# The reciprocal square root of every RMSNorm on 128x5 numbers, spread over the partitions by TensorE

## The chip, the core and the metric

The kernel runs on one core of one Trainium2 chip. The metric is device time in microseconds (us) of one execution; lower is better. The kernel below was timed three times and profiled once more.

## The reference

A two-layer encoder works on 576 tokens at once: 512 of a new stream (`x_prompt`) and 64 of a running one (`x_sample`), each of width 1024. Layer 0 mixes tokens by retention, layer 1 by forgetting attention; both have a half SwiGLU block before and after the mixer. Every projection reads a normalised stream, and one normalisation closes the model:

```python
def rmsnorm(x, g):
    xf = x.astype(jnp.float32)
    y = xf * lax.rsqrt(jnp.mean(xf * xf, axis=-1, keepdims=True) + EPS) * g.astype(jnp.float32)
    return y.astype(x.dtype)

def swiglu_ffn(h, g, w_in, w_out):
    gate, up = jnp.split(rmsnorm(h, g) @ w_in, 2, axis=-1)
    return (jax.nn.silu(gate) * up) @ w_out

h = h + 0.5 * swiglu_ffn(h, ffn1_g, ffn1_w_in, ffn1_w_out)
h = h + mixer(rmsnorm(h, mix_g))            # retention, or forgetting attention
h = h + 0.5 * swiglu_ffn(h, ffn2_g, ffn2_w_in, ffn2_w_out)
# after layer 0 also: k, v, gates = split(rmsnorm(h, kv_g) @ w_kvf)
```

## The kernel before

**Layout.** Activations are kept transposed: `h` is [128 partitions, 8 blocks of the width, 576 tokens], so tokens run along the free dimension. Each projection is cut into units. A unit is 128 output features for all 576 tokens: for each of `kt` blocks of the contraction, TensorE (PE) does three products of split float32 operands (`wl`·`xh`, `wh`·`xl`, `wh`·`xh`), each in two halves of 288 tokens, into two PSUM banks. With 8 blocks that is 48 matmuls. The weights come from HBM into `raw` (SyncE issues the loads), ScalarE (ACT) makes the high part `wh`, VectorE (DVE) the low part `wl`; there are two buffers of `wh`/`wl`, so `wh` of unit u waits for the end of unit u-2.

**The rings.** In the sections named q, k, v and in the retention projections a unit writes one of two pairs of banks (ring of 2), and unit u waits until DVE has taken unit u-2 out of PSUM (semaphore `taken`). In the feed-forward sections the ring has four pairs (`DEEP`). Where a section needs a norm, the sums use banks 4 and 5, so its third unit first waits for a step of the norm (`newton`).

**The norm.** The gain is applied to `h` before the product (`xh`, `xl`), the factor 1/rms after it, when DVE takes a unit out of PSUM: `gate`, `rt`, `kvt`, `qT` are all `ps * rstd`. So `rstd` must stand in SBUF as [128, 576], the same row in every partition. It is made beside the first units of a section:
- GpSimd (POOL) squares and adds the 8 blocks of `h` into `ssq` [128, 576] (L1019, L1023).
- After the first unit PE multiplies `ssq` by a matrix of ones, which sums over the partitions and leaves the sum in every partition (`sum_partitions`, L1195).
- DVE, once it has made `wl` of the third unit, does `make_rstd`: mean plus epsilon out of PSUM (L665), a seed by integer arithmetic (L666), and three Newton steps of three instructions each (L669, L670, L671), all on [128, 576] and each waiting for the one before it. Only then does it take the first unit.

This happens seven times: at the start of ffn1 of layer 0, of the retention projections (the first head only), of ffn2 of layer 0, of k, of q, of ffn2 of layer 1, and for the final norm, behind which there are no more units. ffn1 of layer 1 uses the `rstd` of k again. Below, the norm of ffn1, ffn2 and ffn2 of layer 1 are called norms 0, 2 and 5; those of the retention, k and q norms 1, 3 and 4; the final one is norm 6. The order of instructions on each engine is the order in which the code is written; there is no scheduler. In `section`, DVE and ACT split the weights of unit s+2 ahead of taking unit s.

Of the kernel before, what the change touches and what calls it, by code (L numbers as in the profile page):

```python
# [24 lines left out]
I32 = mybir.dt.int32  # L25
ALU = mybir.AluOpType
# [8 lines left out]
HT = T // 2  # L35
# [12 lines left out]
NEWTON_STEPS = 10  # L48
# [52 lines left out]
def encoder(nc, A, O):  # L101
# [22 lines left out]
    with ExitStack() as ctx:  # L124
# [21 lines left out]
        newt = sb("fixed", "newt", [P, T])  # L146
# [83 lines left out]
        def unit_psum(s, ring=2):  # L230
            return ps[:, 2 * (s % ring):2 * (s % ring) + 2, 0:HT]

        def halves(ap):
            return ap.rearrange("p (a t) -> p a t", a=2)
# [22 lines left out]
        newton = sem("newton")  # L257
        rstd_ready = sem("rstd_ready")
# [387 lines left out]
        def _(dve):  # L646
# [9 lines left out]
            def make_rstd():  # L656

                n_norm[0] += 1
                dve.wait_ge(msum_ready, n_norm[0])

                def step(instruction):
                    n_newton[0] += 1
                    instruction.then_inc(newton, 1)
                    dve.wait_ge(newton, n_newton[0])
                step(nc.vector.tensor_scalar(halves(sq[:, :]), ps[:, 4:6, 0:HT], 1.0 / D, EPS, ALU.mult, ALU.add))  # L665
                step(nc.vector.tensor_scalar(rstd[:, :].bitcast(I32), sq[:, :].bitcast(I32), -0.5, RSQRT_SEED,  # L666
                                             ALU.mult, ALU.add))
                for n in range(3):
                    step(nc.vector.tensor_tensor(newt[:, :], rstd[:, :], rstd[:, :], ALU.mult))  # L669
                    step(nc.vector.scalar_tensor_tensor(newt[:, :], newt[:, :], -0.5, sq[:, :], ALU.mult, ALU.mult))  # L670
                    last = nc.vector.scalar_tensor_tensor(rstd[:, :], newt[:, :], 1.5, rstd[:, :], ALU.add, ALU.mult)  # L671
                    if n < 2:
                        step(last)
                last.then_inc(rstd_ready, 1)
                dve.wait_ge(rstd_ready, n_norm[0])

            def take_h(u, s, j, scale, gain, ring=2):

                dve.wait_ge(unit_done, u + 1)
                nc.vector.scalar_tensor_tensor(halves(h[:, j, :]), unit_psum(s, ring), scale, halves(h[:, j, :]),  # L680
                                               ALU.mult, ALU.add).then_inc(taken, 1)
                if gain is not None:
                    x_tile(j, gain)
# [3 lines left out]
            def ffn(name, gain, factor=None):  # L687
                for part, (j0, n) in enumerate(FF_PARTS):
                    u0, u1, p0 = first[f"{name}_in{part}"], first[f"{name}_out{part}"], pairs[0]

                    def take_in(i, s):
                        b, a = s // 2, p0 + 2 * i + s // 2
                        dve.wait_ge(unit_done, u0 + 4 * i + s + 1)
                        if s % 2 == 0:

                            nc.vector.tensor_tensor(halves(gate[:, b, :]), unit_psum(s, DEEP), halves(rstd[:, :]), ALU.mult) \  # L696
                                .then_inc(taken, 1)
                        else:
                            dve.wait_ge(rsilu_ready, a + 1)
                            nc.vector.tensor_tensor(halves(prod[:, b, :]), unit_psum(s, DEEP), halves(rsilu[:, b, :]), ALU.mult) \  # L700
# [12 lines left out]
            nc.vector.memset(ones[:, :], 1.0).then_inc(setup, 1)  # L713
            dve.wait_ge(const_in, 16 * 8)
# [13 lines left out]
            def head(hd, first_head=False, last_head=False):  # L728
                u0 = RET + 20 * hd

                def scaled(out, s, factor):
                    nc.vector.scalar_tensor_tensor(halves(out), unit_psum(s), factor, halves(rstd[:, :]),
                                                   ALU.mult, ALU.mult).then_inc(taken, 1)
# [110 lines left out]
            def log_gates():  # L844

                dve.wait_ge(f_done, 1)
                step(nc.vector.tensor_tensor(halves(lz[:, :]), ps[0:FOX_HEADS, 4:6, 0:HT], halves(rstd[0:FOX_HEADS, :]),
# [30 lines left out]
            def take_kv(u0, n0):  # L878
                def take(i, s):
# [16 lines left out]
                    nc.vector.tensor_tensor(halves(kvt[:, s % 2, :]), unit_psum(s), halves(rstd[:, :]), ALU.mult) \  # L896
# [16 lines left out]
            def take_q(i, s):  # L913
                dve.wait_ge(unit_done, first["q"] + 4 * i + s + 1)
                nc.vector.scalar_tensor_tensor(halves(qT[:, 4 * i + s, :]), unit_psum(s), (D // FOX_HEADS) ** -0.5,
                                               halves(rstd[:, :]), ALU.mult, ALU.mult).then_inc(taken, 1)
# [241 lines left out]
        def _(pe):  # L1158
            def product(out, terms, start, stop):

                for n, (w, x) in enumerate(terms):
                    for a in range(2):
                        mm = nc.tensor.matmul(out[:, a, :], w, x[:, a * HT:(a + 1) * HT],  # L1163
                                              start=start and n == 0, stop=stop and n == len(terms) - 1)
# [25 lines left out]
            def sum_partitions():  # L1190
# [3 lines left out]
                for a in range(2):  # L1194
                    mm = nc.tensor.matmul(ps[:, 4 + a, 0:HT], ones[:, :], ssq[:, a * HT:(a + 1) * HT], start=True, stop=True)  # L1195
                mm.then_inc(msum_ready, 1)

            def units(name, mh, ml, arrives=None, norm=False, ring=2, after_two=True):
# [37 lines left out]
            pe.wait_ge(setup, 4)  # L1236
            ffn("ffn1_0")

            def head(hd, first_head=False):
                u0 = RET + 20 * hd  # L1240
                for s in range(12):
                    unit(u0 + s, s, KD, xh, xl, x_arrives() if first_head and s == 0 else None)
# [93 lines left out]
            for s in range(4):  # L1336
                unit(u0 + s, s, KD, xh, xl, x_arrives() if s == 0 else None)
# [10 lines left out]
            for k in range(KD):  # L1348
                mm = product(ps[:, 4:6, 0:HT], ((fwl[:, k, :], xh[:, k, :]), (fwh[:, k, :], xl[:, k, :]),
# [121 lines left out]
            sum_partitions()  # L1471

# [37 lines left out]
```

## Time and profile before

| | |
|---|---|
| three runs, us | 2776.21, 2769.71, 2768.78 (median 2769.71) |
| the profiled execution, us | 2764.16 |
| its span, first to last instruction, us | 2762.6 |
| mean granted clock of TensorE | 0.985 of full |
| busy share: PE, DVE, ACT, POOL | 95%, 40%, 24%, 14% |

Between the span and the profiled execution's time lie 1.6 us. The granted clock is 1 where PE runs at full speed (2.4 GHz) and 0.5 at its lower level (1.2 GHz).

### The profile page before, as it was taken

How to read it: one execution, taken by the hardware profiler on the slowest of the kernel's cores; microseconds unless marked ns; L12 is line 12 of the kernel's file. 1: busy time of each engine (PE TensorE's matmuls, PEld its weight loads, DVE VectorE, ACT ScalarE, POOL GpSimd, SP SyncE). 2: the span in 40 equal slices, each digit the busy share in tenths (PEclk: the TensorE clock that was granted, in tenths of full speed). 3: DMA queues.
4: the chain of work that ended last, by engine and by line, in shares of the span. 5: the costliest groups of instructions: out<-in, count | busy, mean ns of one | idle time of the engine just before them, and what ended most of it. 6: DMA issues, size and time to landing. Idle time of an engine off the chain costs nothing.

```text
span 2762.6 us, 44345 instructions
## 1 busy us (share of the span) xinstructions
PE 2624.5 (95%) x18595; PEld 2491.9 (90%) x18595; DVE 1107.2 (40%) x1543; ACT 671.0 (24%) x918; POOL 383.2 (14%) x329
## 2 busy tenths in 40 slices
PE   6999999999899999999999999999998899999995
PEld 5999999969696968999999999999996578999995
DVE  5332335444444446332334433323344545332333
ACT  2221222121212122221222232212213422221220
POOL 3110113101010103100112111001130012100112
PEclk9999999999999999999999999999999999999998
DMA  4232232222221213232233332322331222232220
GB/s 117 84 99 67 79 97 75 61 81 66 72 74 60 83 39 92 84 106 62 84 91 94 113 92 84 96 65 84 92 101 50 78 68 75 82 100 62 84 84 35
DMA packets 392550, 221.74 MB, mean 80 GB/s; under 512 B 8016, under 2 KB 384432, under 8 KB 392416
## 3 DMA queue, kind: packets, MB, share of 16 engines
q1 hardware_dynamic: 387120, 202.82, 25.2%
q0 software_dynamic: 5296, 16.94, 1.9%
q8 instruction: 108, 1.77, 0.3%
q14 instruction: 26, 0.21, 0.0%
HBM read 206.01 MB, written 13.71 MB: 80 GB/s over the span
## 4 chain that ended last, share of the span: by engine, by line
PE 87%; DVE 7%; ACT 2%; issue 1%; DMA 1%; SPq 0%; POOL 0%; DVEq 0%; ACTq 0%; POOLq 0%
PE ps L1163 80%; PE ps L1283 1%; DVE wl L453 1%; PE ps L1296 1%; PE ps L1380 1%; DVE xl L653 1%; PE ps L1271 1%; ACT wh L448 1%; DVE newt L669 1%; DVE rstd L671 1%; DVE newt L670 1%; PE ps L1424 1%; ACT xh L484 1%; DVE sc L921 0%; DVE rt L814 0%
## 5 line engine op out<-in xcount | busy, mean ns | idle before, releaser
L453 DVE TENSOR_TENSOR wl<-raw,wh 128x1024 fp32r<-128x1024 f32 (+3 forms) x352 | 456.9, 1298 | 1347.8 <-ACT wh L448 1347.7
L1163 PE MATMUL ps<-xh,wl 128*128 128x288 f32 x4096 | 885.3, 298 | 23.7 <-DVE xl L653 8.6
L1163 PE MATMUL ps<-xl,wh 128*128 128x288 f32 x4096 | 880.3, 297 | 0.0
L1163 PE MATMUL ps<-xh,wh 128*128 128x288 f32 x4096 | 879.6, 297 | 0.0
L1163 PEld LDWEIGHTS ps<-xh,wl 128*128 128x128 f32 x4096 | 663.9, 190 | 27.7 <-issue 20.1
L448 ACT CAST wh<-raw 128x1024 fp32r<-128x1024 f32 (+3 forms) x352 | 375.7, 1067 | 1263.2 <-PE ps L1163 1262.0
L1163 PEld LDWEIGHTS ps<-xl,wh 128*128 128x128 f32 x4096 | 664.0, 190 | 0.0
L1163 PEld LDWEIGHTS ps<-xh,wh 128*128 128x128 f32 x4096 | 663.6, 190 | 0.0
L1042 POOL TENSOR_TENSOR rsilu<-silu,rstd 128x576 f32<-128x576 f32 x88 | 125.4, 1426 | 1296.4 <-ACT silu L495 1296.4
L1163 PE MATMUL ps<-actl,wh 128*128 128x288 f32 x1408 | 302.0, 295 | 0.0
L1163 PE MATMUL ps<-acth,wh 128*128 128x288 f32 x1408 | 302.0, 295 | 0.0
L1163 PE MATMUL ps<-acth,wl 128*128 128x288 f32 x1408 | 301.9, 295 | 0.0
L1163 PEld LDWEIGHTS ps<-acth,wh 128*128 128x128 f32 x1408 | 225.5, 188 | 0.0
L1163 PEld LDWEIGHTS ps<-actl,wh 128*128 128x128 f32 x1408 | 225.5, 188 | 0.0
L1163 PEld LDWEIGHTS ps<-acth,wl 128*128 128x128 f32 x1408 | 225.5, 188 | 0.0
L495 ACT ACTIVATE silu<-gate 128x576 f32<-128x576 f32 x88 | 60.4, 687 | 197.2 <-DVE gate L696 197.2
L497 ACT CAST acth<-prod 128x576 f32 (+1 forms) x88 | 59.4, 675 | 182.8 <-DVE prod L700 182.8
L703 DVE TENSOR_TENSOR actl<-prod,acth 128x576 f32 (+1 forms) x88 | 66.7, 758 | 78.3 <-ACT acth L497 78.3
L1023 POOL TENSOR_TENSOR ssq<-ssq,sq 128x576 f32<-128x576 f32 x49 | 84.0, 1714 | 3.8
L680 DVE SCALAR_TENSOR_TENSOR h<-ps,h 128x576 f32<-128x576 f32 x104 | 78.0, 750 | 11.7 <-PE ps L1163 11.7
L1019 POOL TENSOR_TENSOR sq<-h 128x576 f32<-128x576 f32 x49 | 56.2, 1147 | 185.4 <-DVE h L680 183.4
L653 DVE SCALAR_TENSOR_TENSOR xl<-h,gains,xh 128x576 fp32r<-128x576 f32 x56 | 58.7, 1068 | 37.1 <-ACT xh L484 37.1
(202 smaller groups left out, 1628.3 us busy)
## 6 DMA issues: line engine op xcount, KB each, us to landing
raw<-in_ffn_w_in SPq DMA_DIRECT2D x176, 512.0 KB, 3.7
raw<-in_ffn_w_out SPq DMA_DIRECT2D x32, 768.0 KB, 4.8
raw<-in_ret_w_in SPq DMA_DIRECT2D x48, 512.0 KB, 3.8
raw<-in_ffn_w_out SPq DMA_DIRECT2D x32, 640.0 KB, 4.4
raw<-in_ret_w_out SPq DMA_DIRECT2D x32, 256.0 KB, 2.7
raw<-in_fox_w_kvf SPq DMA_DIRECT2D x16, 512.0 KB, 4.0
raw<-in_fox_w_q SPq DMA_DIRECT2D x8, 512.0 KB, 4.1
bias<-cum_scratch SPq DMA_DIRECT2D x16, 256.0 KB, 3.2
```

Source lines behind the costliest of these rows:

```text
L448: nc.scalar.copy(wh[:, s % SPLIT, 0:kt, :], raw[:, s, 0:kt, :]).then_inc(hi_ready, 1)
L453: nc.vector.tensor_tensor(wl[:, s % SPLIT, 0:kt, :], raw[:, s, 0:kt, :], wh[:, s % SPLIT, 0:kt, :].bitcast(F32), ALU.subtract).then_inc(lo ...
L484: nc.scalar.activation(xh[:, j, :], h[:, j, :], ACT.Copy, scale=gains[:, gain + j:gain + j + 1]) \
L495: nc.scalar.activation(silu[:, s // 2, :], gate[:, s // 2, :], ACT.Silu).then_inc(silu_ready, 1)
L497: nc.scalar.copy(acth[:, 2 * i + s // 2, :], prod[:, s // 2, :]).then_inc(act_hi, 1)
L653: nc.vector.scalar_tensor_tensor(xl[:, j, :], h[:, j, :], gains[:, gain + j:gain + j + 1], xh[:, j, :].bitcast(F32), ALU.mult, ALU.subtrac ...
L680: nc.vector.scalar_tensor_tensor(halves(h[:, j, :]), unit_psum(s, ring), scale, halves(h[:, j, :]), ALU.mult, ALU.add).then_inc(taken, 1)
L703: nc.vector.tensor_tensor(actl[:, 2 * i + b, :], prod[:, b, :], acth[:, 2 * i + b, :].bitcast(F32), ALU.subtract).then_inc(act_ready, 1)
L1019: nc.gpsimd.tensor_tensor(out[:, :], h[:, j, :], h[:, j, :], ALU.mult).then_inc(sq_step, 1)
L1023: add = nc.gpsimd.tensor_tensor(ssq[:, :], ssq[:, :], sq[:, :], ALU.add)
L1042: nc.gpsimd.tensor_tensor(rsilu[:, b, :], silu[:, b, :], rstd[:, :], ALU.mult) \
L1163: mm = nc.tensor.matmul(out[:, a, :], w, x[:, a * HT:(a + 1) * HT], start=start and n == 0, stop=stop and n == len(terms) - 1)
```

## The change

`sum_partitions` now uses each 128 tokens of `ssq` as the weights and one column of ones as the moving operand, five times. The sum of a token then lies in the partition of the token's number, and all sums form a [128, 5] tile in one bank (for the 64 tokens of the last column only 64 rows). DVE does the same steps on this tile (`nv`, `ny`, `nt`), then multiplies each of five blocks of the identity matrix by one column of the result, which gives `dg` [128, 576] with the factors on diagonals. PE multiplies `dg` by the matrix of ones in the middle of the second unit, ahead of its block 5 (`spread_rstd`), which leaves the row of factors in every partition; DVE copies it from PSUM into `rstd`. In the feed-forward sections the third unit now waits for this copy. In the final norm `spread_rstd` is called straight after the sums.

The two halves of a unit now lie next to each other across the border of two banks (the last 288 columns of one and the first 288 of the next), so that DVE reads 576 columns in one run; `halves` is gone. Sizes of the matmuls are unchanged.

```diff
-HT = T // 2
+TA = 288
+CUTS = ((0, TA), (TA, T))
-NEWTON_STEPS = 10
+SPREAD_AT = 5
-        newt = sb("fixed", "newt", [P, T])
+        dg = sb("fixed", "dg", [P, T])
+        nv, ny, nt = [sb("fixed", n, [P, TT]) for n in ("nv", "ny", "nt")]
         def unit_psum(s, ring=2):
-            return ps[:, 2 * (s % ring):2 * (s % ring) + 2, 0:HT]
+            return pair_psum(2 * (s % ring))
+
+        def pair_psum(bank):
+            end = 512 * (bank + 1)
+            return ps[:, :, :].rearrange("p b c -> p (b c)")[:, end - TA:end - TA + T]
...
-                step(nc.vector.tensor_scalar(halves(sq[:, :]), ps[:, 4:6, 0:HT], 1.0 / D, EPS, ALU.mult, ALU.add))
-                step(nc.vector.tensor_scalar(rstd[:, :].bitcast(I32), sq[:, :].bitcast(I32), -0.5, RSQRT_SEED,
+                nc.vector.tensor_scalar(nv[0:TS, 4:5], ps[0:TS, 4, 4:5], 1.0 / D, EPS, ALU.mult, ALU.add).then_inc(newton, 1)
+                n_newton[0] += 1
+                step(nc.vector.tensor_scalar(nv[:, 0:4], ps[:, 4, 0:4], 1.0 / D, EPS, ALU.mult, ALU.add))
+                step(nc.vector.tensor_scalar(ny[:, :].bitcast(I32), nv[:, :].bitcast(I32), -0.5, RSQRT_SEED,
                                              ALU.mult, ALU.add))
-                for n in range(3):
-                    step(nc.vector.tensor_tensor(newt[:, :], rstd[:, :], rstd[:, :], ALU.mult))
-                    step(nc.vector.scalar_tensor_tensor(newt[:, :], newt[:, :], -0.5, sq[:, :], ALU.mult, ALU.mult))
-                    last = nc.vector.scalar_tensor_tensor(rstd[:, :], newt[:, :], 1.5, rstd[:, :], ALU.add, ALU.mult)
-                    if n < 2:
-                        step(last)
-                last.then_inc(rstd_ready, 1)
+                for _ in range(3):
+                    step(nc.vector.tensor_tensor(nt[:, :], ny[:, :], ny[:, :], ALU.mult))
+                    step(nc.vector.scalar_tensor_tensor(nt[:, :], nt[:, :], -0.5, nv[:, :], ALU.mult, ALU.mult))
+                    step(nc.vector.scalar_tensor_tensor(ny[:, :], nt[:, :], 1.5, ny[:, :], ALU.add, ALU.mult))
+                for t in range(TT):
+                    nc.vector.tensor_scalar(dg[:, P * t:P * t + ROWS[t]], ident[:, 0:ROWS[t]], ny[:, t:t + 1], None, ALU.mult) \
+                        .then_inc(diag_ready, 1)
+                dve.wait_ge(spread, n_norm[0])
+                nc.vector.tensor_copy(rstd[:, :], pair_psum(4)).then_inc(rstd_ready, 1)
                 dve.wait_ge(rstd_ready, n_norm[0])
...
-                for a in range(2):
-                    mm = nc.tensor.matmul(ps[:, 4 + a, 0:HT], ones[:, :], ssq[:, a * HT:(a + 1) * HT], start=True, stop=True)
+                for t in range(TT):
+                    mm = nc.tensor.matmul(ps[0:ROWS[t], 4, t:t + 1], ssq[:, P * t:P * t + ROWS[t]], ones[:, 0:1],
+                                          start=True, stop=True)
                 mm.then_inc(msum_ready, 1)
+
+            def spread_rstd(k):
+
+                if k == SPREAD_AT:
+                    pe.wait_ge(diag_ready, TT * n_norm[0])
+                    for a, z in CUTS:
+                        mm = nc.tensor.matmul(pair_psum(4)[:, a:z], ones[:, :], dg[:, a:z], start=True, stop=True)
+                    mm.then_inc(spread, 1)
...
-                            pe.wait_ge(newton, NEWTON_STEPS * (n_norm[0] - 1) + 1)
-                        unit(u0 + 4 * i + s, s, kt, mh, ml, waits if s == 0 else None, ring, 2 if first_two else None)
+                            pe.wait_ge(rstd_ready, n_norm[0])
+                        unit(u0 + 4 * i + s, s, kt, mh, ml, waits if s == 0 else spread_rstd if waits is not None and norm and s == 1 else None,
+                             ring, 2 if first_two else None)
...
-                unit(u0 + s, s, KD, xh, xl, x_arrives() if s == 0 else None)
+                unit(u0 + s, s, KD, xh, xl, x_arrives() if s == 0 else spread_rstd if s == 1 else None)
...
             sum_partitions()
+            spread_rstd(SPREAD_AT)
```

Where the instructions stand on the engines is shown at three places; line numbers of the changed kernel are its own. VectorE before, at norm 0: the low weight part of the third unit, then the start of the chain, whose three last lines come three times.

```order
L453 TENSOR_TENSOR wl<-raw,wh 128x1024 [waits hi_ready]
L665 TENSOR_SCALAR sq<-ps 128x576 [waits msum_ready]
L666 TENSOR_SCALAR rstd<-sq 128x576 [waits newton]
L669 TENSOR_TENSOR newt<-rstd 128x576 [waits newton]
L670 SCALAR_TENSOR_TENSOR newt<-newt,sq 128x576 [waits newton]
L671 SCALAR_TENSOR_TENSOR rstd<-newt,rstd 128x576 [waits newton]
```

Behind the last L671 stands the taking of the first unit (`gate`). VectorE of the changed kernel at the same place, first the start:

```order
L458 TENSOR_TENSOR wl<-raw,wh 128x1024 [waits hi_ready]
L670 TENSOR_SCALAR nv<-ps 64x1 [waits msum_ready]
L672 TENSOR_SCALAR nv<-ps 128x4
L673 TENSOR_SCALAR ny<-nv 128x5 [waits newton]
L676 TENSOR_TENSOR nt<-ny 128x5 [waits newton]
L677 SCALAR_TENSOR_TENSOR nt<-nt,nv 128x5 [waits newton]
L678 SCALAR_TENSOR_TENSOR ny<-nt,ny 128x5 [waits newton]
```

Then, behind the third L678, VectorE of the changed kernel ends the norm so:

```order
L680 TENSOR_SCALAR dg<-const,ny 128x128 [waits newton]
L680 TENSOR_SCALAR dg<-const,ny 128x128 x3
L680 TENSOR_SCALAR dg<-const,ny 128x64
L683 COPY rstd<-ps 128x576 [waits spread]
L705 TENSOR_TENSOR gate<-ps,rstd 128x576 [waits unit_done,rstd_ready]
L458 TENSOR_TENSOR wl<-raw,wh 128x1024 [waits hi_ready]
```

Eleven instructions on 576 columns became twelve on at most 5, five on 64 or 128, and one on 576 that waits for PE. TensorE between the first and the second unit of the same section, before:

```order
L1163 MATMUL ps<-xh,wh 128x288 x2
L1195 MATMUL ps<-ssq,ones 128x288 [waits ssq_ready]
L1195 MATMUL ps<-ssq,ones 128x288
L1163 MATMUL ps<-xh,wl 128x288 [waits lo_ready]
L1163 MATMUL ps<-xh,wl 128x288
```

The same place in the changed kernel:

```order
L1173 MATMUL ps<-xh,wh 128x288 x2
L1205 MATMUL ps<-ones,ssq 128x1 [waits ssq_ready]
L1205 MATMUL ps<-ones,ssq 128x1 x3
L1205 MATMUL ps<-ones,ssq 64x1
L1173 MATMUL ps<-xh,wl 128x288 [waits lo_ready]
L1173 MATMUL ps<-xh,wl 128x288
```

Two matmuls became five with a moving operand of one column. In the second unit, whose blocks follow each other without a wait before, TensorE of the changed kernel has two more ahead of block 5:

```order
L1173 MATMUL ps<-xh,wh 128x288 x2
L1214 MATMUL ps<-dg,ones 128x288 [waits diag_ready]
L1214 MATMUL ps<-dg,ones 128x288
L1173 MATMUL ps<-xh,wl 128x288 x2
L1173 MATMUL ps<-xl,wh 128x288 x2
```

All later matmuls of the second unit, 18 of them, now stand behind that wait.

## Rows read from the trace of the kernel before

**Rows 1.** The page, section 4: the chain that ended last, by engine and line.
```profile
PE 87%; DVE 7%; ACT 2%; issue 1%; DMA 1%; SPq 0%; POOL 0%; DVEq 0%; ACTq 0%; POOLq 0%
PE ps L1163 80%; PE ps L1283 1%; DVE wl L453 1%; PE ps L1296 1%; PE ps L1380 1%; DVE xl L653 1%; PE ps L1271 1%; ACT wh L448 1%; DVE newt L669 1%; DVE rstd L671 1%; DVE newt L670 1%; PE ps L1424 1%; ACT xh L484 1%; DVE sc L921 0%; DVE rt L814 0%
```

**Rows 2.** Timeline at norms 1, 3, 4: start, duration; idle before, releaser.
```profile
476.66 0.43 PE L1163 MATMUL ps<-xh,wh 128*128 128x288 f32 x2
481.13 0.82 PE L1163 MATMUL ps<-xh,wl 128*128 128x288 f32 x2 [4.04 <-DVE rt L732]
...
477.13 1.04 ACT L448 CAST wh<-raw 128x1024 fp32r<-128x1024 f32 x1 [6.50 <-PE ps L1163]
...
1494.27 1.33 PE L1333 MATMUL ps<-const,kvt 128*128 128x128 f32 x5 [3.99 <-DVE kvt L896]
...
2058.06 0.82 PE L1163 MATMUL ps<-xh,wl 128*128 128x288 f32 x2 [4.09 <-DVE qT L915]
```

**Rows 3.** Timeline of DVE at norms 1 and 5.
```profile
470.66 1.22 DVE L453 TENSOR_TENSOR wl<-raw,wh 128x1024 fp32r<-128x1024 f32 x1 [2.51 <-ACT wh L448]
471.80 0.75 DVE L665 TENSOR_SCALAR sq<-ps 128x576 f32<-128x576 f32 x1
...
480.23 0.76 DVE L732 SCALAR_TENSOR_TENSOR rt<-ps,rstd 128x576 f32<-128x576 f32 x1
...
2309.65 0.75 DVE L665 TENSOR_SCALAR sq<-ps 128x576 f32<-128x576 f32 x1
```

**Rows 4.** Windows from PE's return: length, busy time by engine, granted clock, DMA.
```profile
481.13:486.55 5.42, 5.42 (x22) 5.42 (x23) 5.35 (x5) 0.00 (x0) 3.68 (x2) 0.50 0.34 100
1494.27:1500.31 6.04, 6.04 (x26) 6.00 (x27) 1.89 (x2) 1.69 (x3) 2.22 (x4) 0.50 0.35 108
2058.06:2063.51 5.45, 5.45 (x23) 5.45 (x24) 1.66 (x2) 0.00 (x0) 4.01 (x8) 0.50 0.60 179
```

**Rows 5.** Timeline of PE at norms 2 and 5: start of the fourth unit.
```profile
1076.26 0.53 PE L1163 MATMUL ps<-xh,wl 128*128 128x288 f32 x2 [0.63 <-DVE wl L453]
...
2320.68 0.42 PE L1163 MATMUL ps<-xh,wh 128*128 128x288 f32 x2
2322.19 0.53 PE L1163 MATMUL ps<-xh,wl 128*128 128x288 f32 x2 [1.09 <-DVE wl L453]
```

**Rows 6.** Timeline of DVE and PE at norm 6.
```profile
2729.23 2.29 PE L1195 MATMUL ps<-ssq,ones 128*128 128x288 f32 x4 [3.61 <-POOL ssq L1023]
...
2731.55 0.76 DVE L665 TENSOR_SCALAR sq<-ps 128x576 f32<-128x576 f32 x1 [5.14 <-PE ps L1195]
...
2739.98 1.55 DVE L1000 SCALAR_TENSOR_TENSOR yT<-h,gains,rstd 128x576 f32<-128x576 f32 x2
```

**Rows 7.** Timeline of DVE in retention head 0: eleven chained steps on 128x5.
```profile
571.91 0.17 DVE L792 TENSOR_SCALAR gx<-mv 128x5 f32<-128x5 f32 x1
...
574.13 0.55 DVE L802 TENSOR_SCALAR otok<-otok,mv,gy 128x512 f32<-128x512 f32 x1
```

**Rows 8.** Group of DVE by line and shape: busy us, mean ns.
```profile
L950 DVE TENSOR_SCALAR sc<-sc,rinv 128x128 f32<-128x128 f32 x16 | 4.6, 286 | 0.6
```

**Rows 9.** Timeline of PE: the sums of norm 1, float32 matmuls with new weights.
```profile
469.47 1.24 PE L1195 MATMUL ps<-ssq,ones 128*128 128x288 f32 x4
470.33 0.64 PE L1163 MATMUL ps<-xh,wl 128*128 128x288 f32 x2
...
2128.16 0.44 PE L1391 MATMUL ps<-kTc,qpad_s 128*128 128x128 f32 x2
2128.43 0.33 PE L1392 MATMUL ps<-kTp,qpad_s 128*128 128x64 f32 x2
2128.60 0.19 PE L1393 MATMUL ps<-trisb,idb 128*128 128x64 bf16 x1
```

**Rows 10.** Timeline of PE: block 5 of the second unit at norms 1 and 5.
```profile
474.53 0.43 PE L1163 MATMUL ps<-xh,wl 128*128 128x288 f32 x2
...
2312.14 0.42 PE L1163 MATMUL ps<-xh,wl 128*128 128x288 f32 x2
```

More of the change, by code:

```diff
@@ L679, in take_h @@
                 dve.wait_ge(unit_done, u + 1)
-                nc.vector.scalar_tensor_tensor(halves(h[:, j, :]), unit_psum(s, ring), scale, halves(h[:, j, :]),
+                nc.vector.scalar_tensor_tensor(h[:, j, :], unit_psum(s, ring), scale, h[:, j, :],
                                                ALU.mult, ALU.add).then_inc(taken, 1)
@@ L694, in take_in @@
                         if s % 2 == 0:
-                            nc.vector.tensor_tensor(halves(gate[:, b, :]), unit_psum(s, DEEP), halves(rstd[:, :]), ALU.mult) \
+                            nc.vector.tensor_tensor(gate[:, b, :], unit_psum(s, DEEP), rstd[:, :], ALU.mult) \
                                 .then_inc(taken, 1)
@@ L713, in _ @@
             nc.vector.memset(ones[:, :], 1.0).then_inc(setup, 1)
+            nc.vector.memset(nv[:, :], 1.0).then_inc(setup, 1)
             dve.wait_ge(const_in, 16 * 8)
@@ L731, in scaled @@
                 def scaled(out, s, factor):
-                    nc.vector.scalar_tensor_tensor(halves(out), unit_psum(s), factor, halves(rstd[:, :]),
+                    nc.vector.scalar_tensor_tensor(out, unit_psum(s), factor, rstd[:, :],
                                                    ALU.mult, ALU.mult).then_inc(taken, 1)
@@ L846, in log_gates @@
                 dve.wait_ge(f_done, 1)
-                step(nc.vector.tensor_tensor(halves(lz[:, :]), ps[0:FOX_HEADS, 4:6, 0:HT], halves(rstd[0:FOX_HEADS, :]),
+                step(nc.vector.tensor_tensor(lz[:, :], pair_psum(4)[0:FOX_HEADS, :], rstd[0:FOX_HEADS, :],
                                              ALU.mult))
@@ L895, in take @@
                         dve.wait_ge(kT_stored[s % 2], 16 * min(n // 2, KD // 2))
-                    nc.vector.tensor_tensor(halves(kvt[:, s % 2, :]), unit_psum(s), halves(rstd[:, :]), ALU.mult) \
+                    nc.vector.tensor_tensor(kvt[:, s % 2, :], unit_psum(s), rstd[:, :], ALU.mult) \
                         .then_inc(taken, 1)
@@ L914, in take_q @@
                 dve.wait_ge(unit_done, first["q"] + 4 * i + s + 1)
-                nc.vector.scalar_tensor_tensor(halves(qT[:, 4 * i + s, :]), unit_psum(s), (D // FOX_HEADS) ** -0.5,
-                                               halves(rstd[:, :]), ALU.mult, ALU.mult).then_inc(taken, 1)
+                nc.vector.scalar_tensor_tensor(qT[:, 4 * i + s, :], unit_psum(s), (D // FOX_HEADS) ** -0.5,
+                                               rstd[:, :], ALU.mult, ALU.mult).then_inc(taken, 1)
             section(dve, "q", split_lo, take_q, make_rstd)
@@ L1241, in head @@
                 for s in range(12):
-                    unit(u0 + s, s, KD, xh, xl, x_arrives() if first_head and s == 0 else None)
+                    unit(u0 + s, s, KD, xh, xl, (x_arrives() if s == 0 else spread_rstd if s == 1 else None) if first_head else None)
                     if first_head and s == 0:
```

14 lines of the change are left out of this document (7 added, 7 removed).

## The prediction

> **What bounds the kernel now.** I read the page's chain first: PE makes 87% of it and the product line L1163 alone 80% [rows 1], so a change counts only where PE stands still, where its clock falls, or where it is given work. The chain also holds 1% each of L669, L670 and L671, the Newton steps: somewhere the norm is on the path. The timeline of PE at each norm shows where, and the seven norms are of three kinds.
>
> At norms 1, 3 and 4 the ring has two pairs of banks, and the third unit (or k's transposes) waits until DVE has taken the first. At norm 1 the last pair of matmuls of the second unit starts at 476.66 and ends its turn at 476.92 (0.13 us a matmul); the next starts at 481.13. PE sits idle for 4.04, 3.99 and 4.09 us, and each time what ends the wait is the instruction of DVE that first uses `rstd` [rows 2]. Behind each wait PE comes back at half its clock for 5.42, 6.04 and 5.45 us [rows 4].
>
> At norms 0, 2 and 5 four pairs of banks let PE do three units. At norms 2 and 5 it then waits 0.63 and 1.09 us for the low weights of the fourth [rows 5], and norm 0 looks like norm 2; DVE makes these weights after the chain and the first `gate`.
>
> At norm 6 nothing stands behind the sums: the chain of sums, Newton and the first `yT` is path from 2729.23 to 2739.98, 10.75 us [rows 6].
>
> **The DVE chain.** Before, it takes 8.43 us from L665 at 471.80 to the taking at 480.23 [rows 3]. After, twelve small steps: eleven chained ones on 128x5 take 2.22 us from 571.91 to 574.13, 0.20 each [rows 7]. The twelfth (the second read of the sums, which doesn't wait for the one before) I put at 0.1, together 2.3 us. The five diagonal products have no wait between them. A product of 128x128 by a column lasts 286 ns by itself [rows 8]; how far such instructions overlap the trace doesn't show here, so they cost between 5 x 0.20 (the pitch of the small steps) and 5 x 0.29 = 1.43. I take 1.05, because what is behind the start of the last is one duration, not five. So the diagonals are there 3.35 us (to 3.75) after DVE begins. The copy of `rstd` out of PSUM is one more instruction of 576 columns like L665, 0.75 and 0.04 to the next.
>
> On the small steps the Trainium skill, "VectorE: DVE Perf Modes", section "The TRN2 errata", gives two fixed costs for an instruction, 58 cycles in a table and some 150 as measured. By the first a 128x5 step would last 66 ns, by the second 162 ns. The row shows 0.17 us for L792 [rows 7], so the trace speaks for the second; by the first the diagonals would be ready 1.6 us sooner, PE would never wait for them, and the sum would be near 2752 us.
>
> **PE's own work.** The two old matmuls of the sums occupy PE from 469.47 to 470.33, 0.86 us; each is two float32 pieces. The five new ones are ten pieces with one column, each behind its own weights. The nearest row: four float32 pieces with reloaded weights start between 2128.16 and 2128.60, 0.11 each [rows 9]. They have 128 and 64 columns and the pitch is the same for both, so I take it to be that of the weights: 1.1 us, 0.25 more than now. Bounds: no more than now, or 0.13 each and 0.45 more. The spreading is the same size as the old sums: 0.86, and I take 1.0, since the pair behind them takes 0.64 instead of 0.42.
>
> **Norm 1, as the model of 1, 3 and 4.** DVE begins at 471.80 as now (it is held by the low weights of the third unit, and the sums are done by then). The diagonals are ready at 475.15. PE reaches block 5 of the second unit at 474.53 now [rows 10], at 474.78 then, and waits 0.4 us. All that follows in the unit is later than now by 475.18 - 474.53 + 1.0 = 1.65, so the unit ends at 476.92 + 1.65 = 478.57. The spreading ends at 476.2; with 0.2 until DVE sees it and 0.79 for the copy, the first unit is being taken at 477.2 and is taken at 477.95, 0.6 us before PE asks. So PE goes on at 478.57 and not at 481.13: 2.56 us gained, and three such norms give 7.6. Queued behind the waiting matmul is only the rest of the second unit. Behind DVE's new wait stands the first taking and then the low weights of the fourth unit, which begin once ACT has made the high ones after the second unit's end. Both halves take some 2.3 us (ACT's cast 1.04 [rows 2], DVE's part no longer than 1.22 [rows 3]), so they are there by 481 and needed at 485: 4 us of cover.
>
> Without the wait of 4 us the clock should not fall: in all stretches around the norms of the other kind, with waits of 0.6 to 1.1 us, it stays up. The half-clock stretches are 5.42 + 6.04 + 5.45 = 16.91 us long [rows 4], with PE busy in all of them; the work in them takes half as long at full clock: 8.45 us gained. This is the largest term and the least certain.
>
> **Norms 0, 2 and 5.** Worked out at norm 5: DVE begins at 2309.65 [rows 3], diagonals at 2313.00, block 5 now at 2312.14 [rows 10], so everything behind moves by 0.89 + 1.0 = 1.89. The third unit ends now at 2320.94 (last pair at 2320.68 plus two turns) and then at 2322.83; the fourth starts now at 2322.19 [rows 5]. Its weights are then early, since DVE is done about 3 us sooner. So 0.64 us is lost: a wait of 1.1 us is replaced by work and a wait that are longer. At norms 0 and 2 the idle time won back is 0.5 us less, but DVE begins that much earlier against PE, and the loss is again about 0.6. Together -1.9.
>
> **Norm 6.** All on the path, at half clock [rows 6]. Now 2.32 us from the first sum to L665 and 8.43 of chain. Then 2.32 + 0.3 for the sums, 3.35 of chain, 2.3 for spreading (it is what the sums take now until DVE begins) and 0.79 for the copy: 9.06 against 10.75, 1.7 gained.
>
> **Sum.** 7.6 + 8.45 - 1.9 + 1.7 = 15.8 us. The profiled execution goes from 2764.2 to 2748.4. It lay 5.5 us below the median of the three runs, 2769.71; taking the same 15.8 off that median gives 2753.9. A measurement of this kernel can tell about 0.3%, 8.3 us, from no change: the gain is 0.57%.
>
> **At nothing.** `halves` is gone, the taking L732 lasts 0.76 us on two runs of 288 columns [rows 3] and I take it to last that on one run of 576; even 0.3 us more on each would hide below the 6.6 us of a unit (470.33 to 476.92 [rows 2, 9]) while PE is the bound. One more memset at the start lies beside the loads.
>
> **The rivals.**
> - *The clock falls all the same* (a short wait at block 5 and small matmuls in the sums might be enough). Then 7.4 us remain: profiled 2756.8, median 2762.3, within 0.3%. Against it: around the waits of 0.6 to 1.1 us at norms 2 and 5 no half-clock row appears. Chance 0.12.
> - *The diagonals come much too late*: PE stands at block 5 in six norms, where before it had work. For this VectorE's chain would have to be slowed, by work of GpSimd beside it or by each small step costing more behind a read of PSUM. The break-even is 15.8 / 6 = 2.6 us of lateness at each norm, less if the clock falls for it too: 17 small instructions at 0.35 instead of 0.2. At 3 us of lateness the six norms lose 18, the clock's 8.45 are not won back and 7.4 remain of the gain: 2769.7 + 18 - 7.4 = 2780, slower. Against it: the 128x5 steps were measured, and GpSimd has done its sums when DVE begins. Chance 0.05.
> - *The small steps or the sums are cheaper than taken*: no wait at block 5 saves up to 0.4 us at four norms and 0.15 to 0.6 at the others, 2 us in all: 2752. Chance 0.13.
> - *The cover was not the last wait*: behind norm 1, 3 or 4 another wait (the rope work in the retention, k's stores to HBM, the loads for attention) takes back what is gained, half of the 7.6 and some clock. Median 2758 to 2762. Chance 0.12.
>
> **How the numbers follow.** My forecast, 2750 to 2758, has 0.58. The half-clock stretches elsewhere in the kernel may also come or go with a shift of a few us; each is worth 1.7 to 3.4 us, which widens both sides. The range for 8 in 10 reaches from 2748 to 2762: up to the case of the clock that doesn't recover, down to cheap steps with a lucky clock. Faster by over 0.3% (below 2761.4) takes the forecast, the cheap steps and three quarters of the last rival: 0.80. Within 0.3%: 0.15. Slower: 0.05.
>
> **What would show it.** Right: no idle row over 1 us between the first and the fourth unit of any norm; a wait of 0.1 to 0.6 us ahead of block 5 of the second unit, ended by the diagonal products; granted clock 1.00 in the windows behind norms 1, 3 and 4; the small steps at a pitch of 0.2 us; ten pieces of sums in 1.1 us. Wrong: a third unit that still waits for a taking at norms 1, 3, 4; half-clock windows there; sums that hold PE over 1.5 us; a copy that ends after the second unit does, which would put the chain back on the path.

## The result: 1.2% faster, twice what was forecast

| | before | after |
|---|---|---|
| median, us (lowest to highest) | 2769.24 (2762.16 to 2776.21), 4 runs | 2734.44 (2731.7 to 2739.83), 4 runs |
| profiled execution, us | 2764.16 | 2734.45 |
| its span, us | 2762.6 | 2732.9 |
| granted clock | 0.985 | 0.987 |

The ratio is 0.9883 (95% interval 0.9856 to 0.9909): 32 us less, 25 to 40. The forecast was 15.8 us less and a range down to 2748. The profiled spans lie 29.7 us apart, and the readings below are made on these two.

The page of the changed kernel, first the busy shares, then the chain by engine and by line, as [rows 1]:

```profile
PE 2616.4 (96%) x18665; PEld 2484.6 (91%) x18665; DVE 1077.6 (39%) x1593; ACT 671.6 (25%) x918; POOL 382.5 (14%) x329
...
PE 90%; DVE 5%; ACT 2%; issue 1%; DMA 1%; SPq 0%; POOL 0%; DVEq 0%; ACTq 0%; POOLq 0%
PE ps L1173 82%; PE ps L1303 1%; PE ps L1316 1%; PE ps L1400 1%; DVE wl L458 1%; PE ps L1291 1%; DVE xl L658 1%; PE ps L1444 1%; DVE sc L931 0%; ACT wh L453 0%; DVE rt L824 0%; DMA raw<-in_ffn_w_in 0%; ACT ogh L543 0%; ACT xh L489 0%; ACT sc L595 0%
```

The Newton steps, L669 to L671 before and L676 to L678 now, are gone from the chain, and VectorE's share fell from 7% to 5%. PE at norm 1 in the changed kernel (the timeline, columns as in [rows 2]):

```profile
465.91 1.26 PE L1205 MATMUL ps<-ones,ssq 128*128 128x1 f32 x10
467.10 0.53 PE L1173 MATMUL ps<-xh,wl 128*128 128x288 f32 x2
...
470.93 0.42 PE L1173 MATMUL ps<-xh,wh 128*128 128x288 f32 x2
471.58 1.24 PE L1214 MATMUL ps<-dg,ones 128*128 128x288 f32 x4 [0.23 <-DVE dg L680]
472.44 0.64 PE L1173 MATMUL ps<-xh,wl 128*128 128x288 f32 x2
472.92 0.42 PE L1173 MATMUL ps<-xl,wh 128*128 128x288 f32 x2
...
474.77 0.42 PE L1173 MATMUL ps<-xh,wh 128*128 128x288 f32 x2
475.04 0.43 PE L1173 MATMUL ps<-xh,wl 128*128 128x288 f32 x2
```

The last row is the third unit: it begins 0.27 us behind the pair before it, with no idle time, where [rows 2] had 4.04. From the start of the sums to the third unit are 475.04 - 465.91 = 9.13 us; before, 481.13 - 469.47 = 11.66. That is 2.53 gained, with 2.56 forecast. VectorE at the same norm:

```profile
467.09 1.23 DVE L458 TENSOR_TENSOR wl<-raw,wh 128x1024 fp32r<-128x1024 f32 x1 [2.50 <-ACT wh L453]
468.23 0.14 DVE L670 TENSOR_SCALAR nv<-ps 64x1 f32<-64x1 f32 x1
468.30 0.14 DVE L672 TENSOR_SCALAR nv<-ps 128x4 f32<-128x4 f32 x1
468.47 0.17 DVE L673 TENSOR_SCALAR ny<-nv 128x5 int32<-128x5 int32 x1
...
470.28 0.17 DVE L678 SCALAR_TENSOR_TENSOR ny<-nt,ny 128x5 f32<-128x5 f32 x1
470.49 1.04 DVE L680 TENSOR_SCALAR dg<-const,ny 128x128 f32<-128x128 f32 x5
472.85 0.76 DVE L683 COPY rstd<-ps 128x576 f32<-128x576 f32 x1 [1.33 <-PE ps L1214]
473.65 0.76 DVE L742 SCALAR_TENSOR_TENSOR rt<-ps,rstd 128x576 f32<-128x576 f32 x1
```

The diagonals end at 471.53, 3.30 after the chain's start. The windows behind norms 1, 3 and 4 (length, then busy time and count of PE, PEld, DVE, ACT, POOL, then the granted clock), which answer to [rows 4]:

```profile
473.90:479.30 5.40, 5.40 (x42) 5.40 (x41) 3.46 (x5) 1.05 (x1) 1.01 (x1) 1.00 0.08 20
1483.33:1489.40 6.07, 6.07 (x49) 6.07 (x48) 1.89 (x2) 1.69 (x3) 2.42 (x4) 1.00 0.43 124
2045.00:2051.00 6.00, 6.00 (x47) 6.00 (x46) 1.89 (x2) 1.05 (x1) 0.00 (x0) 1.00 0.90 261
```

The clock is 1.00 where it was 0.50, and 42 matmuls start in the time of 22. Norm 6, PE and then VectorE, as [rows 6]:

```profile
2702.33 1.26 PE L1205 MATMUL ps<-ones,ssq 128*128 128x1 f32 x10 [3.61 <-POOL ssq L1033]
2706.99 2.29 PE L1214 MATMUL ps<-dg,ones 128*128 128x288 f32 x4 [3.40 <-DVE dg L680]
```

```profile
2703.63 0.15 DVE L670 TENSOR_SCALAR nv<-ps 64x1 f32<-64x1 f32 x1 [4.11 <-PE ps L1205]
...
2709.31 0.76 DVE L683 COPY rstd<-ps 128x576 f32<-128x576 f32 x1 [2.38 <-PE ps L1214]
2710.11 5.92 DVE L1010 SCALAR_TENSOR_TENSOR yT<-h,gains,rstd 128x576 f32<-128x576 f32 x8
```

From the sums to `yT` are 7.78 us, where before there were 10.75. Not all went as forecast: at norm 2 PE fell to half clock in the middle of the sums, where before it had stayed up, and the sums held it for 1.57 us (1050.83 to 1052.40). Its sums, the products behind them, and the clock in that stretch:

```profile
1050.83 1.65 PE L1205 MATMUL ps<-ones,ssq 128*128 128x1 f32 x10 [0.21 <-POOL ssq L1033]
1052.40 0.85 PE L1173 MATMUL ps<-xh,wl 128*128 128x288 f32 x2
1053.05 0.68 PE L1173 MATMUL ps<-xl,wh 128*128 128x288 f32 x2
```

```profile
1051.40:1058.20 6.80, 6.80 (x31) 0.50 0.28 80
```

**The part that nobody forecast.** All this explains some 11 us. The rest lies where no norm is. The input projection of each feed-forward block is done in two parts, of 24 and of 20 units, and an output part of 8 units follows each. In the window from 300 to 380, in the second part of ffn1's input projection, PE is busy without a break in both kernels, at full clock (length, PE busy and count, clock, share and GB/s of DMA). Before:

```profile
300.00:380.00 80.00, 80.00 (x602) 1.00 0.30 89
```

After:

```profile
300.00:380.00 80.00, 80.00 (x618) 1.00 0.30 89
```

The same matmuls, 16 more of them in 80 us. Taken start to start in the trace, the products of 288 columns run in one of three steady rhythms: 140, 131, 131, 131 ns and over again (mean 133.3), a pattern of 130 to 135 ns (mean 132.2), or 132, 128 ns (mean 130.0). Before, nearly every section ran at 133.3. After, the second parts of the input projections (80 units) ran at 130.0, and the output parts of the feed-forward blocks and of the retention at 132.2.

The change gives the fixed tiles `nv`, `ny` and `nt` 32 bytes each. That moves every tile allocated behind them by 96 bytes, and `acth`, `actl`, `ogh` and `ogl`, the moving operands of the output projections, from 96 past a multiple of 128 bytes to 64 past one. `xh` and `xl`, ahead of them, stay at a multiple of 128.

Worked out from the starts of the matmuls: how long each part of the program lasts before, and by how much the profiled execution of each kernel differs (us; the other kernels are described below):

```
part                      before   after  a_pad32  b_pad32  b_pad96  b_filler
section of norm 0         194.09   +0.79    +0.41    +0.48    +0.75    -0.16
section of norm 1          84.61   -5.01    -5.00    -0.92    -0.34    -2.44
section of norm 2         155.48   +6.66    +5.12    +3.44    +3.40    +3.37
section of norm 3 (k)     131.63   -4.20    -5.08    -0.30    -1.09    -2.71
section of norm 4 (q)      58.20   -4.14    -4.14    +0.73    -0.05    -1.55
section of norm 5         162.83   +1.49    +1.77    +1.21    +1.54    +1.10
norm 6 to the end          37.28   -2.80    -2.60    -0.67    -0.11    -0.57
4 second parts, input     511.92  -12.72    +0.05     0.00   -12.72     0.00
8 output parts, ffn       563.20   -4.72     0.00    -0.15    -4.72     0.00
first part, ffn1 layer 1  163.29   +0.34    +1.44    +0.02    +1.35    -0.01
rest of the retention     504.31   -2.24    -4.39    -3.43    -0.69    -1.36
attention                 195.77   -3.16    +2.80    -0.11    +2.18    +2.54
sum                      2762.60  -29.71    -9.62    +0.30   -10.50    -1.79
```

The norms' seven rows add up to -7.2 for the changed kernel, but +3.4 in the row of norm 2 and +0.8 in that of norm 4 aren't the norm's: every kernel in this table has them, because the profiled execution of before alone ran these two sections at 130.0 once their first three or four units were done. Without them the norms give -11.4, and the two rows of rhythm -17.4.

### The profile page after: what moved, and what is told of

Read it like the earlier page. It is cut to its first block, busy times and chain, and to the rows that moved or that the text cites. A ratio compares the mean times of both kernels' runs of the same rounds, so it can differ in the third digit from the quotient of the medians.

```text
span 2732.9 us, 44535 instructions
## 1 busy us (share of the span) xinstructions
PE 2616.4 (96%) x18665; PEld 2484.6 (91%) x18665; DVE 1077.6 (39%) x1593; ACT 671.6 (25%) x918; POOL 382.5 (14%) x329
## 4 chain that ended last, share of the span: by engine, by line
PE 90%; DVE 5%; ACT 2%; issue 1%; DMA 1%; SPq 0%; POOL 0%; DVEq 0%; ACTq 0%; POOLq 0%
PE ps L1173 82%; PE ps L1303 1%; PE ps L1316 1%; PE ps L1400 1%; DVE wl L458 1%; PE ps L1291 1%; DVE xl L658 1%; PE ps L1444 1%; DVE sc L931 0%; ACT wh L453 0%; DVE rt L824 0%; DMA raw<-in_ffn_w_in 0%; ACT ogh L543 0%; ACT xh L489 0%; ACT sc L595 0%
## 5 line engine op out<-in xcount | busy, mean ns | idle before, releaser
L1173 PE MATMUL ps<-xh,wl 128*128 128x288 f32 x4096 | 881.1, 297 | 12.8 <-DVE xl L658 8.6
L1173 PE MATMUL ps<-xh,wh 128*128 128x288 f32 x4096 | 876.5, 296 | 0.0
L1173 PE MATMUL ps<-xl,wh 128*128 128x288 f32 x4096 | 876.4, 296 | 0.0
L1173 PEld LDWEIGHTS ps<-xh,wl 128*128 128x128 f32 x4096 | 661.9, 190 | 15.5 <-issue 11.2
L1173 PEld LDWEIGHTS ps<-xl,wh 128*128 128x128 f32 x4096 | 661.3, 189 | 0.0
L1173 PEld LDWEIGHTS ps<-xh,wh 128*128 128x128 f32 x4096 | 661.2, 189 | 0.0
L1173 PE MATMUL ps<-actl,wh 128*128 128x288 f32 x1408 | 300.7, 294 | 0.0
L1173 PE MATMUL ps<-acth,wl 128*128 128x288 f32 x1408 | 300.1, 294 | 0.0
L1173 PE MATMUL ps<-acth,wh 128*128 128x288 f32 x1408 | 298.6, 293 | 0.0
L1173 PEld LDWEIGHTS ps<-acth,wh 128*128 128x128 f32 x1408 | 225.2, 188 | 0.0
L1173 PEld LDWEIGHTS ps<-actl,wh 128*128 128x128 f32 x1408 | 224.8, 188 | 0.0
L1173 PEld LDWEIGHTS ps<-acth,wl 128*128 128x128 f32 x1408 | 224.2, 187 | 0.0
```

What stands on the lines that cost most here:

```text
L1173: mm = nc.tensor.matmul(out[:, a:z], w, x[:, a:z], start=start and n == 0, stop=stop and n == len(terms) - 1)
```

## The experiments

Each ratio is to the kernel before, timed beside it on the same chip.

**Is it the placement?** Unused tiles move what is allocated behind them: `pad = sb("fixed", "pad", [P, 8])` (32 bytes) behind `scrap` in the kernel before (b_pad32) and in the changed one (a_pad32), [P, 16] (b_pad64) and [P, 24] (b_pad96) in the kernel before. b_border makes only the other part of the edit:

```diff
-            return ps[:, 2 * (s % ring):2 * (s % ring) + 2, 0:HT]
+            end = 512 * (bank + 1)
+            return ps[:, :, :].rearrange("p b c -> p (b c)")[:, end - HT:end + HT]
```

> The kernel before, with 32 bytes of SBUF left free behind the fixed tiles, so that acth, actl, ogh and ogl start on a multiple of 64 bytes (before, they start 32 past one, as xh and xl do not). Nothing else changes. Address theory: the matmuls of the out sections go from 133.3 to 132.3 ns start to start, and the second in part of each feed-forward block from 133.0-133.3 to 130.0; 12 to 18 us faster than before. Rival (layout of the units in PSUM): no change within 3 us, out sections stay at 133.3.

> The same with 64 bytes, so that the start of these tiles moves but stays 32 past a multiple of 64. Theory of 64-byte alignment: no change within 3 us, out sections at 133.3 ns. Rival (any move of these tiles can help): faster by 10 us or more.

> The changed kernel, with 32 more bytes, so that acth, actl, ogh and ogl are 32 past a multiple of 64 again, as they were before the change. Address theory: out sections back at 133.3 ns, the second in parts near 133; the gain over before falls to about 16 us, near 2750. Rival (PSUM layout or the order of PE's work): as the changed kernel, 2731 to 2740.

> The kernel before with only the new layout in PSUM: the two halves of a unit on both sides of a bank's border, read by VectorE in one run of 576. The norm stays. PSUM theory: 12 to 18 us faster than before, out sections at 132.3 ns. Address theory: no change within 3 us.

| kernel | median, us | ratio (95%) |
|---|---|---|
| b_pad32 | 2764.41 | 0.9993 (0.9978 to 1.0009) |
| b_pad64 | 2762.26 | 0.9979 (0.9964 to 0.9993) |
| a_pad32 | 2754.18 | 0.9959 (0.9947 to 0.9971) |
| b_border | 2766.77 | 1.0008 (0.9994 to 1.0022) |

b_pad32 missed: a start at a multiple of 128 bytes for `acth` is no better than one at 96 past. So the theory of a 64-byte alignment fell. b_pad64, with `acth` at 32 past, shows no other rhythm either, and its 0.2% is less than can be told from no change here. But 32 bytes more in the changed kernel cost it its gain in rhythm, all of it. The window again, of a_pad32:

```profile
300.00:380.00 80.00, 80.00 (x602) 1.00 0.30 89
```

So a_pad32 is the norm alone: 0.9959, 11.3 us (8 to 15), and the layout across the bank border is worth nothing that can be measured (b_border). What these four leave is a start of exactly 64 past a multiple of 128. Three more kernels test that from both sides: b_pad96 gives the kernel before exactly the changed kernel's placement; in a_x64 64 bytes ahead of `xh` and of `raw` put `xh` and `xl` at 64 too; in a_x64_act0 another 64 behind `scrap` put `acth` and its like back at 0.

> The kernel before, with 96 bytes left free, so that acth, actl, ogh and ogl start where they start in the changed kernel: 64 past a multiple of 128, with xh and xl on a multiple of 128. Norm and PSUM layout are those of before. Placement theory (the start of the moving operand modulo 128 bytes sets the rhythm of the matmuls: 133.3 ns at 0, 132.2 at 64, and an in section entered from the latter stays at 130.0): 14 to 20 us faster than before, near 2749. Rival (it takes the new norm or the new PSUM layout as well): within 5 us of before.

> The changed kernel with xh and xl moved to 64 past a multiple of 128 as well; weights stay on a multiple of 128. Placement theory by the start alone: all sections at 132.2 ns, so the first in parts, the retention, k, v and q gain about 9 us and the second in parts lose about 8: within 4 us of the changed kernel. Rival (what counts is a difference between sections): another rhythm.

> The changed kernel with the two placements exchanged: xh and xl 64 past a multiple of 128, acth, actl, ogh, ogl on a multiple of 128. Placement theory: in sections at 132.2 ns, out sections, entered from them, at 130.0: some 12 us faster than the changed kernel, near 2722. Rival: xh and xl at 64 don't change the in sections, and the out sections go back to 133.3: 2750.

| kernel | median, us | ratio (95%) |
|---|---|---|
| b_pad96 | 2754.27 | 0.9940 (0.9921 to 0.9960) |
| a_x64 | 2733.13 | 0.9865 (0.9847 to 0.9882) |
| a_x64_act0 | 2733.84 | 0.9867 (0.9843 to 0.9891) |

b_pad96 computes as before does, with one unused tile, and gains 0.6%: 16.6 us. Its window:

```profile
300.00:380.00 80.00, 80.00 (x618) 1.00 0.30 89
```

With the norm's 11.3 that is 27.9 us, within the interval of the 32. In a_x64 the input sections, which read `xh` and `xl` at 64, all ran at 132.2, and no tile but these two lies otherwise within 128 bytes than in the changed kernel: it is the start of the moving operand that counts, not that of another tile. In the first part of ffn1 (60 to 160) the kernel before has the first row, a_x64 the second:

```profile
60.00:160.00 100.00, 100.00 (x752) 1.00 0.29 85
```

```profile
60.00:160.00 100.00, 100.00 (x759) 1.00 0.29 83
300.00:380.00 80.00, 80.00 (x607) 1.00 0.28 83
```

The first part went from x752 to x759, and the second back from x618 to x607: a start at 64 gives 132.2 everywhere, a start at 0 gives 133.3 or 130.0. The sum hardly changes. In a_x64_act0 the output parts, now at 0, split in the same way: the first ones at 133.3, the second at 130.0. It had been expected near 2722, with all of them at 130.0; 2733.84 is a miss.

**Can 130.0 be had everywhere?** In the changed kernel a second part of the input projection follows an output part, at 132.2, and gets 130.0, the first gets 133.3. a_kick puts twelve matmuls whose moving operand starts at 64 ahead of the fourth unit of each first part, as if to hand over the rhythm:

```diff
+            def kick(k):
+                if k == 0:
+                    for _ in range(12):
+                        nc.tensor.matmul(ps[:, 6, 224:512], xh[:, 0, 0:P], xh[:, 0, 16:16 + TA], start=True, stop=True)
```

> The changed kernel; in the first four units of each first in part TensorE does 12 more matmuls ahead of the fourth unit, whose moving operand starts 64 past a multiple of 128 (1.6 us, result overwritten). Theory that the rhythm is kept from what ran before: the remaining 20 units or so of the four first in parts run at 130.0 instead of 133.3 ns, 3.2 us each, less 1.6 for the kick: about 6 us faster than the changed kernel, near 2728. Rival (the rhythm belongs to the section): 6 us slower, near 2741, in sections still at 133.3.

2744.39 us, 0.9909 (0.9886 to 0.9933). It missed: the first parts stayed at 133.3, so a short run of such matmuls hands nothing over.

a_cut272 makes the halves 272 and 304 columns, so that the second half starts at 64 where the first starts at 0:

```diff
-TA = 288
+TA = 272
```

> The changed kernel with a unit cut into 272 and 304 tokens instead of 288 and 288. The number of columns is the same, but the second moving operand of each pair now starts 64 bytes past a multiple of 128 where the first starts on one (and the reverse cannot occur). Placement theory by the start of each operand: in sections leave the 133.3 ns rhythm for a mean of 132.2 or less; between 0 and 20 us faster than the changed kernel. Rival (the start matters only by the section's tiles): no change within 3 us.

2730.04 us, 0.9867 (0.9842 to 0.9892). All input sections ran at 131.7 (k's and v's at 131.8), with no dependence on what went before. In the output parts it is the first half that starts at 64 and the second that starts at 0; they ran at 132.7. a_cut272_act0 adds a pad of 64 bytes behind `scrap`, so that the output operands too start at 0:

> The changed kernel cut into 272 and 304 tokens, with 64 bytes left free so that acth, actl, ogh and ogl start on a multiple of 128 as xh and xl do. Placement theory by the start of each operand: the out sections, at 132.6 ns with the same cut and a start at 64, come to the 131.4 of the in sections: 5,000 matmuls by 1.1 ns, 5 to 6 us faster than with the cut alone, near 2724, and faster than both kernels. Rival (the first operand at 64 is as good): within 3 us of the cut alone.

2729.1 us, 0.9854 (0.9838 to 0.9871). The step happened: the eight output parts ran at 131.7, and lasted 7.1 us less than before in place of 2.8 for the cut alone. The time doesn't show it: 2729.1 against 2730.04, and the ratios' intervals overlap. Up to the last product the trace has 58 us at half clock, that of a_cut272 41. A product takes 240 ns at half clock and 131.7 here at full, so these 17 us cost some 7.7, more than the 4 won. It is the lowest median of the study, but that it beats the changed kernel (0.9883) is not shown.

**The clock.** b_filler is the kernel before with 28 matmuls, whose result nothing reads, in the wait at norms 1, 3 and 4. PE stays busy there and nothing else changes:

```diff
+            def filler():
+                for _ in range(28):
+                    nc.tensor.matmul(ps[:, 6, 0:HT], xh[:, 0, 0:P], xh[:, 0, 0:HT], start=True, stop=True)
```

> The kernel before; during the wait for the norm's chain at norms 1, 3 and 4 TensorE does 28 matmuls on data at hand into a free bank (3.7 us of the 4.2 idle). Their result isn't used. Theory that the idle stretch makes the clock fall: no half-clock stretch behind norms 1, 3 and 4, and 6 to 9 us faster than before, though the path has no less work. Rival (the clock falls for another reason, or the half-clock stretches cost nothing): within 2 us of before or slower.

2763.75 us, 0.9982 (0.9968 to 0.9996): 5 us, between 1 and 9. Its timeline at norm 1, and the windows from PE's return at the three norms:

```profile
476.76 3.85 PE L1201 MATMUL ps<-xh 128*128 128x288 f32 x28
480.96 0.49 PE L1163 MATMUL ps<-xh,wl 128*128 128x288 f32 x2 [0.35 <-DVE rt L732]
```

```profile
480.96:486.40 5.44, 5.44 (x41) 1.00 0.34 96
1493.80:1499.80 6.00, 6.00 (x47) 1.00 0.44 128
2056.50:2062.00 5.50, 5.50 (x43) 1.00 0.74 224
```

It was the idling: with PE busy through the wait the clock stays at 1.00, and 41 matmuls start where 22 did [rows 4]. The table has -2.44, -2.71 and -1.55 at these norms, 6.7 together, and 7.5 with the 0.8 of norm 4's row that is the rhythm's. The 5 us lie under the 6 to 9 that were expected, but their interval reaches up to 9.

**The wait at block 5.** a_spread6 moves the spreading one block back (`SPREAD_AT = 6`).

> The changed kernel with the spreading ahead of block 6 of the second unit instead of block 5, 0.8 us later. The wait of 0.5 to 0.8 us for the diagonal products at block 5 should vanish, and the copy still end before the second unit does: 0.5 us less at each of five norms, 2 to 3 us in all. Rival: the copy gets late, the third unit waits for the first taking at norms 1, 3 and 4, no gain.

2735.44 us, 0.9884 (0.986 to 0.9908), the changed kernel's own ratio. Of PE and then of VectorE at norm 1:

```profile
471.00 1.13 PE L1214 MATMUL ps<-dg,ones 128*128 128x288 f32 x4
...
473.29 0.43 PE L1173 MATMUL ps<-xh,wh 128*128 128x288 f32 x2
473.87 0.50 PE L1173 MATMUL ps<-xh,wl 128*128 128x288 f32 x2
```

```profile
472.17 0.76 DVE L683 COPY rstd<-ps 128x576 f32<-128x576 f32 x1 [1.54 <-PE ps L1214]
472.96 0.76 DVE L742 SCALAR_TENSOR_TENSOR rt<-ps,rstd 128x576 f32<-128x576 f32 x1
```

The wait ahead of L1214 is gone, but the third unit starts 0.58 behind the last pair instead of 0.27, once L742 has taken the first. At norms 1, 3 and 4 the wait moved by one place. At norms 0 and 5, where four pairs of banks leave room, the stretch up to the fifth unit is 0.3 and 0.7 us shorter than in the changed kernel; all five together give 1.6 us, too little to be seen in the times.

## Why the prediction was half right

**The chain.** 3.30 us to the last diagonal, forecast 3.35. The pitch of the small steps is 0.20, as [rows 7]; the second read starts 0.07 behind the first and its follower 0.17 later, 0.24 for the pair where 0.30 was taken. The five diagonals start 0.20 apart and take 1.04, forecast 1.05, though each lasts 0.28 as in [rows 8].

**Sums and spreading.** The ten pieces hold PE from 465.91 to 467.10, 1.19 us, forecast 1.1 and at most 1.3 by its own bounds. The spreading holds it from 471.58 to 472.44, 0.86, and the pair behind it takes 0.48 instead of 0.27: 1.07 in all, forecast 1.0.

**The wait at block 5.** 471.58 is 0.65 behind the start of the last pair; without a wait it would be 0.27, so 0.38 were waited, forecast 0.4.

**Norms 1, 3 and 4.** The idle rows are gone. Norm 1 gave 2.53 of 2.56.

**The clock.** Right in kind: behind these three norms it is 1.00, and b_filler shows that the idling caused the half. The size of the term was a little too large, by one step: that the work takes half as long at full clock. The kernel before, behind norm 1, within the stretch of [rows 4]:

```profile
484.15 0.68 PE L1163 MATMUL ps<-xh,wl 128*128 128x288 f32 x2
484.63 0.68 PE L1163 MATMUL ps<-xl,wh 128*128 128x288 f32 x2
```

Two products start every 0.48 us, so one takes 240 ns at half clock, where it takes 133.3 at full: 0.56 and not 0.5 of it. So 16.91 us at half clock cost 7.5 and not 8.45, and b_filler's rows in the table, with the 0.8 of norm 4's rhythm, come to the same 7.5.

Norm 2 of the changed kernel shows why such a term isn't safe: there a stretch of half clock came that wasn't there before, 6.8 us long, which costs some 3, and its sums held PE for 1.57 us, over the 1.5 that the prediction named as a sign of being wrong. A fall at this place came in four of the eight kernels with the new norm (the changed one, a_pad32, a_x64, a_cut272_act0) and in none of the six with the old one; what decides is open. The rival of the clock that falls all the same came true at one norm where it hadn't been looked for, not at the three.

**Norms 0, 2 and 5.** -1.9 was forecast, 0.64 at norm 5 and about as much at the others. From the last start in the first unit to the first in the fifth, norms 0 and 5 took 21.63 us before and 22.22 in the changed kernel: 0.6 lost at each, as forecast, and the fourth unit starts without a wait. At norm 2 it was 21.52 and 24.93, 3.4 lost: the same 0.6 and, for nearly all the rest, the half clock.

**Norm 6.** 2.97 gained, forecast 1.7. The chain to PE's spreading was 3.36, the spreading to the copy 2.32 and the copy 0.80, all three as forecast (3.35, 2.3, 0.79). The sums took 1.30 up to L670 and not 2.62: at norm 6 of the changed kernel PE still ran at full clock when they began, and half clock came only behind them. The 1.3 us above the forecast are that luck.

**The sum.** Taken in the same way, from the first unit to the fifth, norms 1, 3 and 4 gave 5.01, 5.21 and 4.77, 15.0 together where 7.6 + 8.45 was forecast. With 4.6 lost at norms 0, 2 and 5 and 3.0 gained at norm 6 that makes 13.4 us at the norms, against the 15.8 of the forecast: 0.9 is the clock term, 2.7 norm 2's clock, and norm 6 gave 1.3 back. The norm alone was measured at 11.3 us, with an interval of 8 to 15 (a_pad32), which holds the 13.4; the table's 11.4 also holds what the clock did later in these sections.

**The step that failed** is the one under "At nothing": it put everything else that the change does at no cost and no gain, and named the layout, `halves` and the memset. The layout is indeed worth nothing (b_border). But it overlooked that three small tiles in the fixed region move the addresses of the tiles allocated behind them. That alone is worth 16.6 us (b_pad96, 11 to 22), at least as much as the norm: by the table 17.4 against 11.4, while the intervals of the times overlap. The Trainium skill, "SBUF — State Buffer", section "Operand start alignment", asks for a start at a multiple of the element's size only, and says that its runs timed nothing, so it gives no price for a placement. The trace shows that placement within that rule moves the rhythm by up to 2.5% (130.0 against 133.3 ns). The Trainium skill, "VectorE: DVE Perf Modes", section "The TRN2 errata — SBUF-src ops pay a fixed extra latency per instruction", has a row for matmuls of 6 cycles and one for each column. The estimate from it for 288 columns is 294 cycles, 122.5 ns at 2.4 GHz; the three rhythms lie 7.5 to 11 ns above.

**What stays open.** Why a moving operand that starts at 64 past a multiple of 128 bytes gets 132.2 and one at 32 or 96 133.3, and why at 0 there are two rhythms. What picks between them isn't simply what ran before: in a_kick twelve matmuls didn't do it, and in a_spread6 the parts of ffn1 in layer 1 swapped (the first at 130.0, -3.72 us against before, the second at 133.3) with all addresses as in the changed kernel. That weight loads and moving reads meet in SBUF would fit all of it, but is only argued: no run here changed the placement of `wh` and `wl` by themselves. The differences of the attention (-3.2 to +2.8 us in the table) and of the rest of the retention (-0.7 to -4.4) are not explained either; they come and go between kernels that do the same there. In the first part of ffn1 in layer 1 they are the clock: it is at half for 6.8 us in before and the changed kernel, and for 10.2 in a_pad32 and b_pad96, the two that are 1.4 us longer there.

## What to carry to other kernels

A cross-partition reduction whose result is one number per token is best kept at one number per token: eleven steps on 576 columns became twelve on at most 5, and TensorE can spread the result in the middle of a unit that it has to do anyway. A change that allocates anything, however small, changes two things; time it once with a pad that puts the addresses back (a_pad32), and the old kernel once with the new addresses (b_pad96). In a kernel where PE is 96% busy, look at the pitch of its steadiest loop before anything else: 17,328 products run in L1173, and one nanosecond of each is 17.3 us.

## What was unexpected of the hardware

- Products of 288 columns with new weights each run at a mean pitch of 133.3, 132.2 or 130.0 ns, each steady over dozens of units. With the moving operand at 64 past a multiple of 128 bytes it was 132.2, at 32 or 96 past 133.3, at 0 either 133.3 or 130.0. With halves of 272 and 304 columns it was 131.7 where the first starts at 0 and the second at 64, and 132.7 the other way round.
- Addresses alone don't fix the rhythm: the profiled execution of before ran norm 2's section at 130.0, 3.4 us faster than b_pad32, b_pad96 and b_filler, whose `xh` and `xl` lie at the same place and whose norm is the same. Whether two executions of one kernel can differ so is not shown: each was profiled once.
- Ten float32 pieces of one column with new weights, of 128x128 at most, take 1.19 us at full clock, as long as nine products of 288 columns.
- A product of 288 columns takes 240 ns start to start at half clock and 133.3 at full, so full clock saves 0.44 of the time at half and not 0.5.
